# Merge and output projection of a block in three fp32r passes of split halves, with GpSimd making two of the low halves

## What is computed

```python
def merge_branches(y_a, y_b, g_logits, w_pa, w_pb, w_o):
    g_a, g_b = jnp.split(g_logits, 2, axis=-1)
    mixed = jax.nn.sigmoid(g_a) * (y_a @ w_pa) + jax.nn.sigmoid(g_b) * (y_b @ w_pb)
    return mixed @ w_o
...
        x_mix, _, _ = token_mixer(hx @ w_in[l], lbs[l], s_f, s_b, *mix_args)
        x = x + gt1 * x_mix
```

## Time and profile before

| | |
|---|---|
| median of 3 runs | 2044.93 us (2038.69 to 2046.03) |
| the profiled execution, its own time | 2046.49 us |
| its span in the trace | 2044.7 us |
| mean granted TensorE clock | 0.980 of full |
| busy: PE, PE weight loads | 1948.5 us (95%), 1407.9 us (69%) |
| busy: DVE, ACT, POOL | 729.5 us (36%), 610.5 us (30%), 399.6 us (20%) |

### The profile page before, as it was taken

One profiled execution on the slowest core, in us unless ns is written; L12 is line 12 of the kernel. 1 busy time (PEld: TensorE's weight loads), 2 busy tenths in 40 slices (PEclk: granted clock), 3 DMA queues, 4 the chain that ended last, 5 costly groups with the idle time before them and its releaser, 6 DMA issues.

```text
span 2044.7 us, 27449 instructions
## 1 busy us (share of the span) xinstructions
PE 1948.5 (95%) x11522; PEld 1407.9 (69%) x11522; DVE 729.5 (36%) x1209; ACT 610.5 (30%) x931; POOL 399.6 (20%) x209
## 2 busy tenths in 40 slices
PE   6999899999999999997999899999999999888998
PEld 2767687874444444445787657777777778678998
DVE  1624235232222222226243754222222535474333
ACT  2422102022222222223111634322223511445454
POOL 2000000020000000005000521433333310434764
PEclk9999989989999999998999999999999999999999
DMA  9469916449999999983222202544444223413541
GB/s 358 161 219 362 338 42 226 178 178 367 426 424 424 424 427 421 423 358 117 83 96 96 89 31 91 194 148 144 153 174 147 84 83 124 167 42 143 187 176 52
DMA packets 120213, 428.38 MB, mean 210 GB/s; under 512 B 5690, under 2 KB 23141, under 8 KB 107456
## 3 DMA queue, kind: packets, MB, share of 16 engines
q1 hardware_dynamic: 118016, 416.56, 52.8%
q0 software_dynamic: 2112, 10.57, 1.4%
HBM read 426.07 MB, written 1.05 MB: 209 GB/s over the span
## 4 chain that ended last, share of the span: by engine, by line
PE 64%; PEld 18%; issue 7%; DVE 4%; ACT 3%; POOL 2%; DMA 2%; PEldq 0%; DVEq 0%; POOLq 0%; SPq 0%; ACTq 0%
PE bank L527 62%; PEld bank L527 18%; PE bank L542 2%; DMA ring<-in_ada_w 1%; DMA ring<-in_w_in 1%; DVE H L1913 1%; DVE H_low L1920 0%; PEldq L506 0%; POOL arena L1822 0%; POOL arena L1821 0%; POOL arena L1826 0%; POOL arena_r L1868 0%; POOL arena L1824 0%; POOL arena L1827 0%; DVE H L2401 0%
## 5 line engine op out<-in xcount | busy, mean ns | idle before, releaser
L527 PE MATMUL bank<-arena_r 128*128 128x512 f32 (+1 forms) x2112 | 599.5, 351 | 12.8 <-ACT arena_r L1339 5.4
L527 PE MATMUL bank<-arena_r,ring_low 128*128 128x512 f32 (+2 forms) x1792 | 561.3, 347 | 5.4 <-DVE H_low L1920 5.3
L527 PEld LDWEIGHTS bank<-arena_r 128*128 128x128 f32 x2112 | 374.5, 190 | 105.1 <-issue 48.7
L527 PEld LDWEIGHTS bank<-arena_r,ring_low 128*128 128x128 f32 (+1 forms) x1792 | 329.0, 189 | 51.5 <-issue 6.1
L527 PE MATMUL bank<-arena 128*128 128x64 bf16 (+8 forms) x2588 | 311.6, 287 | 29.9 <-DMA arena<-in_hy_filt_w 11.6
L527 PEld LDWEIGHTS bank<-arena 128*128 128x128 bf16 (+4 forms) x2588 | 194.2, 135 | 133.5 <-issue 96.6
L527 PE MATMUL bank<-ring,arena 128*64 128x512 f32 x1024 | 278.2, 594 | 1.1 <-ACT arena L1508 0.7
L527 PE MATMUL bank<-H_low,arena_r 128*128 128x512 f32 (+1 forms) x672 | 216.0, 338 | 0.0
L2464 DVE SCALAR_TENSOR_TENSOR X<-bank,mod,X 128x256 f32<-128x256 f32 x216 | 94.6, 479 | 315.9 <-PE bank L527 315.9
L1353 ACT ACTIVATE arena<-bank 128x512 f32<-128x512 f32 (+2 forms) x106 | 51.4, 496 | 411.9 <-PE bank L527 411.8
L1854 POOL TENSOR_TENSOR ring_low<-ring,arena_r 128x2048 fp32r<-128x2048 f32 x32 | 146.9, 4611 | 129.1 <-ACT arena_r L1698 71.3
(11 more groups left out here) (287 smaller groups left out, 1982.0 us busy)
## 6 DMA issues: line engine op xcount, KB each, us to landing
ring<-in_moe_w_gate SPq DMA_DIRECT2D x32, 2048.0 KB, 13.6
ring<-in_w_mlp SPq DMA_DIRECT2D x32, 2048.0 KB, 8.8
ring<-in_w_in SPq DMA_DIRECT2D x26, 2048.0 KB, 8.1
ring<-in_ada_w SPq DMA_DIRECT2D x24, 2048.0 KB, 13.3
ring<-in_moe_w_up SPq DMA_DIRECT2D x17, 2048.0 KB, 9.2
H<-in_moe_w_down SPq DMA_DIRECT2D x16, 2048.0 KB, 16.0
arena<-in_moe_w_up SPq DMA_DIRECT2D x15, 2048.0 KB, 9.2
ring<-in_moe_w_down SPq DMA_DIRECT2D x15, 2048.0 KB, 16.1
```

What stands on the lines that cost most here:

```text
L527: ins = nc.tensor.matmul(o, l, r, start=start, stop=stop, skip_group_check=True)
```

## The change

The projections of the merge and the output projection go from `mm` to `mm3`. What is needed for that:

- ACT copies the high half of each of the four weight chunks in two pieces of 128x2048 (`merge_high`): MERGE and MERGE+1 between gate tiles, MERGE+2 ahead of the barrier, MERGE+3 behind it.
- DVE subtracts for the low halves of MERGE and MERGE+1 (`merge_low`), one after each product of spectra.
- POOL subtracts for the low halves of MERGE+2 and MERGE+3, behind the barrier and behind its three transfers, four instructions of 128x2048.
- DVE splits `OS`, `YB` and each mixed tile: a copy for the high half, a subtraction for the low one. Per mixed tile that is two instructions more.
- `MT` moves to a small buffer of two tiles, and the modulation vectors move from ahead of the barrier to behind the eight mixed tiles.
- The remaining edits renumber semaphore counts.

```diff
-        MT = A3(17408, KT, L)
+        MT = mrow[0].rearrange("p (a b) -> p a b", a=2)
+        OSh, YBh = AR3(1024, HYT, L), AR3(2048, HYT, L)
+        OSl, YBl = AR3(0, HG_H, L), AR3(12288, HYT, L)
+        MIXh, MIXl = AR3(17408, KT, L), AR3(15360, KT, L)
...
             def merge(nt, side):
...
-                    mm(ps[nt % 4][:, side * L:(side + 1) * L], as_rows(MERGE + side)[:, k, nt * P:(nt + 1) * P], (OS, YB)[side][:, k, :],
-                       k == 0, k == 3, "merge_mm" if (side, k) == (1, 3) else None)
-
-            chunk_in(MERGE)
+                    wh = MERGEh[side][k // 2].rearrange("p (k n) -> p k n", k=2)
+                    mm3(ps[nt % 4][:, side * L:(side + 1) * L], (wh[:, k % 2, c], wl[:, k, c]), (high[:, k, :], lower[:, k, :]),
+                        k == 0, k == 3, "merge_mm" if (side, k) == (1, 3) else None)
+
+            pe.wait_ge(S("w_split"), 5 + 1)
...
-            chunk_in(MERGE + 1)
+            pe.wait_ge(S("w_split"), 5 + 2)
...
-                mm(ps[4 + t % 2][:, 0:L], as_cols(n)[:, k, (t % 4) * P:(t % 4 + 1) * P], MIX[:, k, :], k == 0, k == KT - 1,
-                   "out_mm" if k == KT - 1 else None)
-
-            chunk_in(MERGE + 2)
+                mm3(ps[4 + t % 2][:, 0:L], (wh[:, k % 4, c], as_cols(n, slot=low)[:, k, c]), (MIXh[:, k, :], MIXl[:, k, :]),
+                    k == 0, k == KT - 1, "out_mm" if k == KT - 1 else None)
+
+            pe.wait_ge(S("pool_ready"), 1)
...
-                    chunk_in(MERGE + 3)
+                    pe.wait_ge(S("pool_ready"), 2)
...
+            def merge_high(m):
+                act.wait_ge(full[(MERGE + m) % RING], arrived(MERGE + m))
+                for a in range(2):
+                    A_(MERGEh[m][a], slot(MERGE + m)[:, 2048 * a:2048 * (a + 1)], ACT.Copy).then_inc(S("high_copied"), 1)
+
             gate_tiles(10, 2)
-            gate_tiles(12, 4)
+            merge_high(0)
+            gate_tiles(12, 2)
+            act.wait_ge(S("y_spec"), 2)
+            merge_high(1)
+            gate_tiles(14, 2)
             ada_rows(6, 6, 0)
+            merge_high(2)
             phase_end(act, "hyena")
+            merge_high(3)
             tables()
...
             bring(WR, tall(T["wr"]), "tables_in")
+            for m in (2, 3):
+                for a in range(2):
+                    c = slice(2048 * a, 2048 * (a + 1))
+                    pool.wait_ge(S("high_copied"), 2 + 2 * m + a + 1)
+                    i = G.tensor_tensor(low(MERGE + m)[:, c], slot(MERGE + m)[:, c], MERGEh[m][a].bitcast(F32), ALU.subtract)
+                i.then_inc(S("pool_ready"), 1)
             add_squares(1, L)
...
+            link(V.tensor_copy(OSh, OS))
+            V.tensor_tensor(OSl, OS, OSh.bitcast(F32), ALU.subtract)
+
+            def merge_low(m):
+                for a in range(2):
+                    c = slice(2048 * a, 2048 * (a + 1))
+                    dve.wait_ge(S("high_copied"), 2 + 2 * m + a + 1)
+                    i = V.tensor_tensor(low(MERGE + m)[:, c], slot(MERGE + m)[:, c], MERGEh[m][a].bitcast(F32), ALU.subtract)
+                i.then_inc(S("w_split"), 1)
...
                 dve.drain().then_inc(S("y_spec"), 1)
+                merge_low(f)
...
             link(V.tensor_tensor(YB, UV, CV[:, 8:12, :], ALU.mult))
+            link(V.tensor_copy(YBh, YB))
+            V.tensor_tensor(YBl, YB, YBh.bitcast(F32), ALU.subtract)
+            phase_end(dve, "hyena")
+
+
+            for nt in range(KT):
+                dve.wait_ge(S("merge_mm"), nt + 1)
+                o = ps[nt % 4]
+                V.tensor_tensor(MIX[:, nt, :], GL[:, nt, :], o[:, 0:L], ALU.mult)
+                link(V.tensor_tensor(MT[:, nt % 2, :], GL[:, 8 + nt, :], o[:, L:2 * L], ALU.mult))
+                link(V.tensor_tensor(MIX[:, nt, :], MIX[:, nt, :], MT[:, nt % 2, :], ALU.add))
+                link(V.tensor_copy(MIXh[:, nt, :], MIX[:, nt, :]))
+                V.tensor_tensor(MIXl[:, nt, :], MIX[:, nt, :], MIXh[:, nt, :].bitcast(F32), ALU.subtract).then_inc(S("merged"), 1)
             take_chunk(1, 6, 6, 32, 4)
...
-            phase_end(dve, "hyena")
-
-
-            for nt in range(KT):
-                dve.wait_ge(S("merge_mm"), nt + 1)
...
```

More of the change, by code:

```diff
@@ L407, in build @@
         MIX = A3(15360, KT, L)
-        MT = A3(17408, KT, L)
+        MT = mrow[0].rearrange("p (a b) -> p a b", a=2)
+        OSh, YBh = AR3(1024, HYT, L), AR3(2048, HYT, L)
+        OSl, YBl = AR3(0, HG_H, L), AR3(12288, HYT, L)
+        MIXh, MIXl = AR3(17408, KT, L), AR3(15360, KT, L)
+        MERGEh = [[flat[:, 0:2048], flat[:, 2048:4096]] for flat in (Hl[:, :, :].rearrange("p k n -> p (k n)"), ar_r[:, 21504:25600])]
+        MERGEh += [[ar_r[:, 8192:10240], ar_r[:, 13312:15360]], [ar_r[:, 10240:12288], ar_r[:, 19456:21504]]]
         HB = A(0, 3072).bitcast(BF16).rearrange("p (n b d) -> p n b d", n=3, b=TB)
@@ L809, in merge @@
             def merge(nt, side):
+                c = slice(nt * P, (nt + 1) * P)
+                wl = as_rows(MERGE + side, slot=low)
+                high, lower = ((OSh, OSl), (YBh, YBl))[side]
                 for k in range(4):
-                    mm(ps[nt % 4][:, side * L:(side + 1) * L], as_rows(MERGE + side)[:, k, nt * P:(nt + 1) * P], (OS, YB)[side][:, k, :],
-                       k == 0, k == 3, "merge_mm" if (side, k) == (1, 3) else None)
-            chunk_in(MERGE)
+                    wh = MERGEh[side][k // 2].rearrange("p (k n) -> p k n", k=2)
+                    mm3(ps[nt % 4][:, side * L:(side + 1) * L], (wh[:, k % 2, c], wl[:, k, c]), (high[:, k, :], lower[:, k, :]),
+                        k == 0, k == 3, "merge_mm" if (side, k) == (1, 3) else None)
+            pe.wait_ge(S("w_split"), 5 + 1)
             pe.wait_ge(S("tile_free"), tiles[0])
@@ L831, in merged_out @@
                 n = MERGE + 2 + t // 4
-                mm(ps[4 + t % 2][:, 0:L], as_cols(n)[:, k, (t % 4) * P:(t % 4 + 1) * P], MIX[:, k, :], k == 0, k == KT - 1,
-                   "out_mm" if k == KT - 1 else None)
-            chunk_in(MERGE + 2)
+                c = slice((t % 4) * P, (t % 4 + 1) * P)
+                wh = MERGEh[2 + t // 4][k // 4].rearrange("p (k n) -> p k n", k=4)
+                mm3(ps[4 + t % 2][:, 0:L], (wh[:, k % 4, c], as_cols(n, slot=low)[:, k, c]), (MIXh[:, k, :], MIXl[:, k, :]),
+                    k == 0, k == KT - 1, "out_mm" if k == KT - 1 else None)
+            pe.wait_ge(S("pool_ready"), 1)
             for k in range(KT):
@@ L937, in expert @@
                         mm(ps[2 * tb + nb], PICK[:, tb * P:(tb + 1) * P], YSl[:, s], False, False)
-            pe.wait_ge(S("pool_ready"), 1)
+            pe.wait_ge(S("pool_ready"), 3)
             pe.wait_ge(S("onehot"), 1)
@@ L994, in _ @@
                 if k == 0:
-                    pe.wait_ge(S("pool_ready"), 2)
+                    pe.wait_ge(S("pool_ready"), 4)
                 mm(ps[1][:, 0:L], FIN2[:, k, :], H[:, k, 0:L], k == 0, k == KT - 1, "sum_ready" if k == KT - 1 else None)
@@ L1280, in mlp_pair @@
                                 n += 1
-                        pe.wait_ge(S("w_split"), 5 + 8 * l + j + 1)
+                        pe.wait_ge(S("w_split"), 7 + 8 * l + j + 1)
                         for nt, ks in [(t, (0, 1, 2)) for t in range(3)] + [(t, (3,)) for t in range(3)] + [(t, (0, 1, 2, 3)) for t in range(3, KT)]:
@@ L1805, in _ @@
             G.tensor_copy(low(L0 + 1), slot(L0)).then_inc(S("pool_ready"), 1)
-            pool.wait_ge(S("pool_ready"), 3)
+            pool.wait_ge(S("pool_ready"), 5)
             G.tensor_tensor(low(L0), slot(L0), low(L0 + 1).bitcast(F32), ALU.subtract).then_inc(full[(L0 + 1) % RING], 16)
@@ L2314, in _ @@
                         s = slice(2048 * a, 2048 * (a + 1))
-                        dve.wait_ge(S("high_copied"), 4 + 2 + a + 1)
+                        dve.wait_ge(S("high_copied"), 12 + 2 + a + 1)
                         i = V.tensor_tensor(low(n)[:, s], slot(n)[:, s], NEXTh[2 + a].bitcast(F32), ALU.subtract)
@@ L2471, in _ @@
                 for a in range(2):
-                    dve.wait_ge(S("high_copied"), 2 + 6 * l + a + 1)
+                    dve.wait_ge(S("high_copied"), 10 + 6 * l + a + 1)
                     i = V.tensor_tensor(YTl[a][:, :, 0:W], YT[:, 4 * a:4 * a + 4, 0:W], YTh[:, 4 * a:4 * a + 4, 0:W].bitcast(F32), ALU.subtract)
@@ L2499, in mlp_pair @@
                                 s = slice(2048 * a, 2048 * (a + 1))
-                                dve.wait_ge(S("high_copied"), 4 + a + 1)
+                                dve.wait_ge(S("high_copied"), 12 + a + 1)
                                 i_ = V.tensor_tensor(low(L1)[:, s], slot(L1)[:, s], NEXTh[a].bitcast(F32), ALU.subtract)
```

## The result

| | before | changed |
|---|---|---|
| median of 8 runs | 2042.84 us (2038.69 to 2046.03) | 2051.10 us (2047.84 to 2055.65) |
| ratio, 95% interval | | 1.0046 [1.0036, 1.0057] |
| span of the profiled execution | 2044.7 us | 2046.1 us |
| PE's restart behind the barrier to the closing sums | 49.45 us | 59.85 us |
| `ada_turn` (eight records of 128x8) to that restart | 8.20 us | 7.05 us |

A forecast was written before the change was run, and what follows sets the result against it. PE was taken to bound the kernel; its 9.2 us gain would be more than lost to DVE waiting for POOL. 2046.49 + 5.6 = 2052.1 us profiled, 1.6 us above the median, so 2050.5; range 2035 to 2058.

The forecast's parts named there:

- The matmuls: Merge and output projection: three float32r matmuls at 0.360 us replace one float32 at 0.432, 128 times, 9.2 us less PE work.
- Ahead of the barrier: Before PE's restart: ACT's copies and DVE's subtractions cost nothing; restart at 377.0 instead of 378.1; up to 1 us at risk.
- The conflict and its place: Behind the barrier: POOL's four 4.62 us subtractions hold up DVE's SBUF addition and subtraction, not PSUM readers; PE idles 11.8 us.
- So they alternate, one instruction each: Behind the barrier: waiting DVE and POOL take turns by instruction; first mixed tile at 394.5, closing sums 5.6 us later.
- rival B: Behind the barrier: POOL's four subtractions keep DVE out until 397.9; sums at 437.8, 10.2 us slower, 2055.1 us; chance 0.18.
- The clock: PE after its idle wait: half speed for tile 4, 5.8 us to 400.4, then tiles 5 to 7 at full speed.
- rival D: Merge after PE's idle time: clock stays low through tiles 4 to 7; 14.2 us slower, 2059.1 us; chance 0.11.
- The copy: DVE's 128x256 copy per mixed tile: taken as 0.3 us and as waiting for POOL; otherwise the sum is 0.6 us lower.
- Rivals A and C: A: POOL hardly holds DVE up, 9.2 us faster (0.12); C: one mixed tile per POOL instruction, 2.5 us slower (0.12).

## Why the prediction was right, and where it was wrong

The time came out right, 2050.5 forecast and 2051.1 measured, but partly by luck: the mechanism was one of the rivals. The loss against the kernel before was forecast as 5.6 us and is 7.4 to 11.6 by the interval.

- **The matmuls**: right. The third product costs what the earlier trace rows said; without POOL the stage is 41.46 us, forecast 41.4.
- **Ahead of the barrier**: right. `ada_turn` to restart went from 8.20 to 7.05 us, 1.15 less as forecast; neither ACT nor DVE came last.
- **The conflict and its place**: right. DVE's first addition was stopped 0.11 us behind POOL's first subtraction. That instructions which read PSUM keep their times beside POOL is shown by the variants and not by the changed kernel, where they hardly met it: 0.41 us at 391.33 and 391.66 with the gaps in, and the additions to `X` with POOL run later.
- **The step that failed** is "So they alternate, one instruction each. I take that." POOL's four instructions held DVE out as one, 17.95 us. That is rival B (0.18), whose stage was worked out as 60.8 us and measured as 59.85. The rows it rested on the earlier trace rows were not like the new case: L1769 is in `add_squares`, where POOL waits for its own previous instruction and for ACT before each addition, so a gap was always there. Nor were two instructions waiting when the first L2501 of those rows ended, at 1611.46: DVE's next one started at 1612.17, so POOL's turn in between decided nothing. The run with such a wait put into the changed kernel gave the forecast's turns, at 54.94 us against a forecast of 433.2 - 377.0 = 56.2. A run of subtractions with DVE waiting was in no row of before; I put the turns in its place.
- **The clock**: forecast as half speed for tile 4 alone, 24 records 0.240 us apart. It was tile 4 and three records more, 0.214 apart (392.95 to 398.88); rival D fell. I had it hidden behind DVE's second tile. With POOL's run over, DVE made a tile every 1.91 us, PE's slow tile was in the way, and it cost 2.5 us.
- **The copy**: taken as 0.3 us, is 0.29; taken to contend, does.
- Rivals A and C fell with the 18.12 us.

The forecast number came near because the executions of this kernel scatter by 8 us and because I set out from a median of three, 2044.93, which eight runs put at 2042.84. By the medians the loss is 8.3 us: the forecast loss was 2.7 us short and its start 2.1 us high, and the 0.6 us between 2050.5 and 2051.1 is what is left.

## What to carry to other kernels

Before giving POOL a run of two-input instructions on SBUF, list what DVE does beside it. An addition with two inputs in SBUF stood still for the whole run here, not for one instruction of it; a copy in SBUF was held for one instruction of POOL, and behind a whole run it wasn't tried. If the run must be there, cut it into small pieces with a wait between them that POOL really has to wait for, its own last piece (stage 48.6 us instead of 59.9). Better, let it start when DVE works from PSUM only, or give the work to DVE in its own gaps, which was as good here (41.5 and 41.6).

Don't carry it to every instruction of POOL. In the kernel before, DVE multiplied two regions of the arena beside two `tensor_scalar` of POOL, which read SBUF and follow each other without a gap, and took as long as it did alone:

```profile
1120.52 1.67 POOL L1821 TENSOR_SCALAR arena<-arena 128x512 f32<-128x512 f32 x1 [148.26 <-ACTq L506]
1122.17 1.59 POOL L1822 TENSOR_SCALAR arena<-arena 128x512 f32<-128x512 f32 x1
...
1121.64 0.68 DVE L2358 TENSOR_TENSOR arena<-arena 128x512 f32<-128x512 f32 x1
...
1145.75 0.68 DVE L2358 TENSOR_TENSOR arena<-arena 128x512 f32<-128x512 f32 x1
```

So a rule that any reading instruction of POOL holds a two-input one of DVE goes further than these rows; no run took this case apart.

And when an observed case is to show how two engines share something, check that its instructions follow each other as closely as in the new one.

## What was not expected of the hardware

- The lock outlasts an instruction: four subtractions back to back held one DVE instruction of 0.42 us for 18.12 us, sixteen for 18.59. A gap of 0.08 us between each two of the four was enough for DVE to get in, and its instructions then took 4.0 to 4.8 us each.
- POOL's subtraction of 128x2048 took 3.57 us with source and target the same float32 region, 4.5 to 4.6 from two regions into float32r; which of the two differences does it was not tried.
- Four memsets in a row held no DVE addition. They held one copy to the end of the running memset, 0.33 us, and the three memsets with a copy at their beginning took 0.16 us longer than the first.
